# A conformer/S5/MoE decoder trunk on one core: VectorE instead of TensorE forms four modulation tiles during the feed-forward stage

## The reference, cut to what matters

```python
D_MODEL, SEQ, DEPTH = 1024, 256, 2          # BATCH 1, D_FF_DENSE 2816
cond = jax.nn.silu(c.astype(F32))           # c: (1, 1024)
h = x                                       # (1, 256, 1024)
for i in range(DEPTH):
    mod = cond @ mod_w[i].astype(F32) + mod_b[i].astype(F32)        # (1, 6 * 1024)
    sh1, sc1, g1, sh2, sc2, g2 = jnp.split(mod[:, None, :], 6, axis=-1)
    y = rms_norm(h, norm1_g[i]) * (1.0 + sc1) + sh1
    y = conformer_conv(y, ...) if i == 0 else s5_layer(y, ...)
    h = h + g1 * y
    y = rms_norm(h, norm2_g[i]) * (1.0 + sc2) + sh2
    y = (silu(y @ w_gate) * (y @ w_up)) @ w_down if i == 0 else moe_swiglu(y, ...)   # top 2 of 8 experts
    h = h + g2 * y
return rms_norm(h, final_norm_g)
```

## Time and profile before

| | |
|---|---|
| median of 3 runs | 1613.69 us (1611.99 to 1618.89) |
| the profiled execution's own time | 1611.64 us |
| its span | 1608.9 us |
| mean granted clock of TensorE | 0.975 |
| TensorE busy (PE) | 1514.5 us, 94% |
| VectorE busy (DVE) | 1286.9 us, 80% |
| ScalarE busy (ACT) | 1023.9 us, 64% |
| GpSimd busy (POOL) | 217.3 us, 14% |
| instructions | 23502 |

### The profile page before, as it was taken

How to read it: one execution, slowest core, us unless ns; L and a number is a source line. 1 busy time by engine, 2 the same in 40 slices (tenths; PEclk the granted TensorE clock), 3 DMA queues, 4 the chain that set the end, 5 groups by cost and what they waited for, 6 DMA issues and landing times.

```text
span 1608.9 us, 23502 instructions
## 1 busy us (share of the span) xinstructions
PE 1514.5 (94%) x8591; PEld 1260.1 (78%) x8591; DVE 1286.9 (80%) x1426; ACT 1023.9 (64%) x1045; POOL 217.3 (14%) x251
## 2 busy tenths in 40 slices
PE   6997999998889699999999999999989999999996
PEld 4776899998659678888888888888877777777774
DVE  4796566556875598898899889889868988899886
ACT  4556555455123487687777687777748777778773
POOL 0771146521770000000000000000000000000000
PEclk9998999999789899999999999999999999999998
DMA  9954386656484689999999999999818999999991
GB/s 307 331 195 168 106 284 231 236 193 236 158 262 148 220 315 367 361 340 370 363 341 357 374 350 355 365 351 354 306 53 314 340 338 344 340 313 338 376 379 40
DMA packets 231208, 463.30 MB, mean 288 GB/s; under 512 B 18255, under 2 KB 57687, under 8 KB 231127
## 3 DMA queue, kind: packets, MB, share of 16 engines
q1 hardware_dynamic: 229591, 461.55, 80.6%
q10 hardware_dynamic: 1536, 0.68, 0.2%
HBM read 461.15 MB, written 1.05 MB: 287 GB/s over the span
## 4 chain that ended last, share of the span: by engine, by line
PE 75%; DVE 11%; ACT 4%; POOL 4%; issue 3%; DMA 1%; SPq 1%; DVEq 0%; ACTq 0%; POOLq 0%
PE bank L2163 12%; PE bank L2166 12%; PE bank L2169 12%; PE bank L1823 12%; DVE wlo L1744 4%; PE bank L1978 3%; PE bank L2305 3%; PE bank L2302 3%; PE bank L2257 2%; PE bank L2258 2%; PE bank L2265 2%; PE bank L2270 2%; PE bank L2269 2%; DVE bank L1315 2%; PE bank L1907 2%
## 5 line engine op out<-in xcount | busy, mean ns | idle before, releaser
L1597 DVE TENSOR_TENSOR wlo<-ring,whi 128x2048 fp32r<-128x2048 f32 x210 | 477.0, 2289 | 68.5 <-PE bank L2169 55.6
L1020 ACT ACTIVATE whi<-ring 128x2048 fp32r<-128x2048 f32 x210 | 400.9, 1918 | 117.7 <-PE bank L2166 117.7
L1744 DVE TENSOR_TENSOR wlo<-ring,whi 128x2048 fp32r<-128x2048 f32 x126 | 283.1, 2281 | 26.2 <-PE bank L2270 25.0
L1117 ACT ACTIVATE whi<-ring 128x2048 fp32r<-128x2048 f32 x126 | 238.4, 1912 | 37.7 <-PE bank L2265 22.9
L2163 PE MATMUL bank<-whi,xe_hi 128*128 128x512 f32 x560 | 219.7, 392 | 7.2 <-ACT whi L1020 7.2
L2166 PE MATMUL bank<-whi,xe_lo 128*128 128x512 f32 x560 | 218.9, 391 | 0.0
L1233 DVE TENSOR_TENSOR ring_lo<-ring,ehi 128x2048 fp32r<-128x2048 f32 x45 | 106.3, 2362 | 58.3 <-ACT ehi L786 58.2
L2169 PE MATMUL bank<-wlo,xe_hi 128*128 128x512 f32 x560 | 150.5, 391 | 0.0
L2163 PEld LDWEIGHTS bank<-whi,xe_hi 128*128 128x128 f32 x560 | 105.8, 189 | 29.4 <-issue 7.3
L2169 PEld LDWEIGHTS bank<-wlo,xe_hi 128*128 128x128 f32 x560 | 105.7, 189 | 22.1
L2166 PEld LDWEIGHTS bank<-whi,xe_lo 128*128 128x128 f32 x560 | 105.8, 189 | 21.9
(11 more groups left out here) (450 smaller groups left out, 2829.4 us busy)
## 6 DMA issues: line engine op xcount, KB each, us to landing
ring<-in_moe_w_gate_dram SPq DMA_DIRECT2D x112, 1024.0 KB, 7.1
ring<-in_moe_w_up_dram SPq DMA_DIRECT2D x112, 1024.0 KB, 6.8
ring<-in_moe_w_down_dram SPq DMA_DIRECT2D x112, 1024.0 KB, 6.7
ring<-in_mod_w_dram SPq DMA_DIRECT2D x24, 2048.0 KB, 9.8
ring<-in_ffn_w_gate_dram SPq DMA_DIRECT2D x11, 1024.0 KB, 6.1
ring<-in_ffn_w_up_dram SPq DMA_DIRECT2D x11, 1024.0 KB, 8.7
ring<-in_ffn_w_down_dram SPq DMA_DIRECT2D x11, 1024.0 KB, 5.2
ring<-in_conv_w_pw_dram SPq DMA_DIRECT2D x8, 1024.0 KB, 12.3
```

Source lines behind the costliest of these rows:

```text
L1020: act.activation(whi[:, n % HI_SLOTS, :], ring[:, s * HW:(s + 1) * HW], ACT.Copy).then_inc(hi_ready, 1)
L1117: act.activation(whi[:, q % HI_SLOTS, :], ring[:, s * HW:(s + 1) * HW], ACT.Copy).then_inc(hi_ready, 1)
L1597: v.tensor_tensor(wlo[:, n % LO_SLOTS, :], ring[:, s * HW:(s + 1) * HW], whi[:, n % HI_SLOTS, :].bitcast(F32), ALU.subtract).then_inc(lo_r ...
L1744: v.tensor_tensor(wlo[:, q % LO_SLOTS, :], ring[:, s * HW:(s + 1) * HW], whi[:, q % HI_SLOTS, :].bitcast(F32), ALU.subtract).then_inc(lo_r ...
```

## The change

VectorE computes tiles 12 to 15. It multiplies the 512 columns of each of the 8 row tiles by that row tile's values of `cond_late`, one per partition, and adds them up in PSUM bank 6, in 8 steps (`mod_products`); the last step writes to SBUF, where `mod_copy` used to write. The first four steps stand behind `hid_lo` of half 2b, the last four behind `hid_lo` of half 2b+1, ahead of the tables. TensorE's `mod_partial` and ScalarE's `mod_copy` of these tiles are gone. `mod_sums` stays on TensorE, now against a column of ones, and moves from the end of block b to the end of block b+1; `mod_vector` moves likewise. `mod_part`, on which SP waits for the tile's slot, is now counted up by VectorE's last step. The counts of `mod_acc` behind these tiles are four lower (`copies_after`).

```diff
@@ -468,6 +468,13 @@
         S5_TABLE_ORDER = [(2 * m + k) * 4 + q for m in range(4) for q in range(4) for k in range(2)]
         TABLES_AT = [0, 4, 4] + [3] * 8
 
+        def by_vector(m):
+            return 2 * FFN_MODS <= m < 2 * S5_MODS
+
+        def copies_after(m):
+
+            return m - sum(by_vector(k) for k in range(m))
+
         def mod_place(m):
 
             if m < 2 * FFN_MODS:
@@ -933,16 +940,13 @@
                     if f >= 4:
                         act.wait_ge(down_used, f - 3)
                     act.activation(hid_hi[:, f % 4, :], hid[:, f % 4, :], ACT.Copy).then_inc(hidhi_ready, 1)
-                if b in FFN_MOD_BLOCKS:
-                    m = 2 * FFN_MODS + FFN_MOD_BLOCKS.index(b)
-                    mod_copy(m)
                 for n in range(TABLES_AT[b]):
                     if 0 < b < FBLOCKS - 1 and n == TABLES_AT[b] - 1:
                         split_hi(UNIT[("down", b - 1, 0)] + 2)
                     sin_tables(made)
                     made += 1
-                if b in FFN_MOD_BLOCKS and m % 2:
-                    mod_vector(m // 2)
+                if b - 1 in FFN_MOD_BLOCKS[1::2]:
+                    mod_vector(FFN_MODS + FFN_MOD_BLOCKS.index(b - 1) // 2)
 
             squares(hT, sq, h3_ready, lambda kc: kc + 1)
             root(3)
@@ -1356,6 +1360,24 @@
             mod_bias(NORM_MODS + 1)
 
 
+            def mod_products(m, kcs):
+
+                n = WHERE[("mod", m)]
+                w, acc_, dst = early(n, KC), psum[6][:, :], mod_place(m)[2]
+                for kc in kcs:
+                    cc = cond_late[:, kc, 0:1]
+                    if kc == 0:
+                        v.wait_ge(cond_ready, 2)
+                        v.wait_ge(mod_acc, 2 * FFN_MODS)
+                        v.wait_ge(arr[slot_of(n)], arrived_count(n))
+                        link(v.tensor_scalar(acc_, w[:, kc, :], cc, None, ALU.mult))
+                    elif kc < KC - 1:
+                        link(v.scalar_tensor_tensor(acc_, w[:, kc, :], cc, acc_, ALU.mult, ALU.add))
+                    else:
+                        v.wait_ge(mod_sum, m)
+                        v.scalar_tensor_tensor(dst, w[:, kc, :].rearrange("p (a n) -> p a n", a=2), cc,
+                                               acc_.rearrange("p (a n) -> p a n", a=2), ALU.mult, ALU.add).then_inc(mod_part, 1)
+
             made = 0
             for b in range(FBLOCKS):
                 for f in (2 * b, 2 * b + 1):
@@ -1368,6 +1390,8 @@
                     v.wait_ge(hidhi_ready, f + 1)
                     v.tensor_tensor(hid_lo[:, f % 4, :], hid[:, f % 4, :], hid_hi[:, f % 4, :].bitcast(F32),
                                     ALU.subtract).then_inc(hidlo_ready, 1)
+                    if b in FFN_MOD_BLOCKS:
+                        mod_products(2 * FFN_MODS + FFN_MOD_BLOCKS.index(b), range(4 * (f % 2), 4 * (f % 2) + 4))
                 for _ in range(TABLES_AT[b]):
 
                     i = S5_TABLE_ORDER[made]
@@ -1899,7 +1923,7 @@
                 bank = mod_place(m)[0]
                 pe.wait_ge(arr[slot_of(n)], arrived_count(n))
                 if m >= 2:
-                    pe.wait_ge(mod_acc, m - 1 if 2 <= m < 2 * FFN_MODS else m)
+                    pe.wait_ge(mod_acc, m - 1 if 2 <= m < 2 * FFN_MODS else copies_after(m))
                 w, cc = early(n, KC), cond if m < 2 * FFN_MODS else cond_late
                 for first in (True, False):
                     for j in range(4):
@@ -1914,10 +1938,13 @@
                 k, h = m // 2, m % 2
                 if k and h == 0:
                     pe.wait_ge(mod_raw, k)
-                pe.wait_ge(mod_acc, m + 1)
+                if by_vector(m):
+                    pe.wait_ge(mod_part, m + 1)
+                else:
+                    pe.wait_ge(mod_acc, copies_after(m + 1))
                 for o in range(4):
                     ins = mm(bank[:, 4 * h + o:4 * h + o + 1], part[:, o // 2, (o % 2) * P:(o % 2) * P + P],
-                             sum_col[:, :], start=True, stop=True)
+                             ones[:, 0:1] if by_vector(m) else sum_col[:, :], start=True, stop=True)
                 ins.then_inc(mod_sum, 1)
 
             def mod_tiles(first, last):
@@ -1992,15 +2019,11 @@
                         ins = split_product(psum[4 + f % 2][:, g * T:(g + 1) * T], u, y_hi, g,
                                             2 if f == 0 and g == 0 else None)
                     ins.then_inc(gu_done, 1)
-                if b in FFN_MOD_BLOCKS:
-                    m = 2 * FFN_MODS + FFN_MOD_BLOCKS.index(b)
-                    pe.wait_ge(cond_ready, 2)
-                    pe.wait_ge(var_ready, 3)
-                    mod_partial(m)
                 if b:
                     down(b - 1)
-                if b in FFN_MOD_BLOCKS:
-                    mod_sums(m)
+                if b - 1 in FFN_MOD_BLOCKS:
+                    pe.wait_ge(var_ready, 3)
+                    mod_sums(2 * FFN_MODS + FFN_MOD_BLOCKS.index(b - 1))
             down(FBLOCKS - 1)
             pe.wait_ge(mod_raw, S5_MODS)
             sums(3 * KC, sq_ready, sq, sum_ready)
```

## The result

| | before | after |
|---|---|---|
| median | 1613.17 us (5 runs, 1611.93 to 1618.89) | 1629.39 us (5 runs, 1626.77 to 1630.66) |
| ratio | | 1.0094, 95% interval 1.0078 to 1.0109: 15 us slower |
| span of the profiled execution | 1608.9 us | 1628.6 us |
| mean granted clock | 0.975 | 0.963 |

One of the eight executions of the kernel with four steps in half 2 (under Experiments) took 2517.89 us at a mean granted clock of 0.555, and its figures leave that one out.

A forecast was written before the change was run, and what follows sets the result against it. The prediction took the feed-forward stage as TensorE-bound and serial. Its terms, 0 + 3.0 + 1.7 + 2.9 = +7.6 us, plus 3.4 for the clock, gave +11.0 on 1611.64: 1623 us, range 1615 to 1631.

The forecast's parts named there:

- Points 1 to 3: Feed-forward stage: TensorE loses 7.40 us, VectorE gains steps of 0.78 us, its chain comes 3.3 us late against 0.7 slack.
- point 2: Steps added to VectorE: 0.78 us each, 3.1 us for four, from a 746 ns row rather than a 698 ns estimate.
- Point 4: Blocks 6 and 8: stretch 20.1 us against 20.2, change 0, as the removed 1.85 us comes back as a wait.
- Point 5: Block 2: chain held by GpSimd, end of unit 2 at 254.8 instead of 251.8, change +3.0 us.
- Point 6: Block 4: chain held by GpSimd at hid_lo of half 1, stretch 21.9 us against 20.2, change +1.7 us.
- Point 7: Four sums of 0.79 us move into blocks 3, 5, 7 and 9, where TensorE is the bound: +2.9 us.
- Point 8: TensorE's clock: one half-rate spell each in blocks 2 and 4, none in 6 and 8, +3.4 us, bounds 0 and 6.8.
- Point 9: DMA: tile slots freed later, nothing counted, at worst 1 us in each of the four blocks.
- only shifted: All stages behind the feed-forward stage would start later but otherwise stay unchanged.
- Rival A: Waits come but no clock spells, or steps take 0.70 us: +5 to +8, 1616.5 to 1619.5 us; chance 0.24.
- rival C: Faster: the last four steps hide, leaving only the 7.40 us removed from TensorE, 1604 us; chance 0.07.
- B's late transfers: Rival with everything late, 1630 us: transfers late by 1 us per block (4 more), spells in all four blocks; chance 0.11.

The follow-up runs named there:

- the kernel with four steps in half 2: Changed kernel without row tiles 3 to 6 of the four modulation tiles, its four steps per tile all in half 2; 1620.78 us, ratio 1.0041.
- The run with the clock kept up: Changed kernel plus idle TensorE passes at the old place, three portions in block 2, two in 4, one in 6 and 8; 1622.09 us, ratio 1.0051.
- the run with the tables first: Changed kernel with the last four steps behind the tables, ahead of the block's last ring_lo, nothing left out; 1619.38 us, ratio 1.0031.

## Why the prediction was right, and where a size was off

The direction, the place and the mechanism were right, and the time lay in the range; against the 11.0 us forecast, the measured difference was 15.

- Points 1 to 3. TensorE's 7.4 us vanish in waits of its own: shown by putting them back, which costs nothing in blocks 6 and 8 and nothing on balance in the stage. Steps 743 to 755 ns (0.75 taken). The estimate of 698 ns that point 2 works out from the Trainium skill (page "VectorE: DVE Perf Modes", section "Side-by-side: where the cycles go for N=2048 bf16") was 0.05 us too low; the trace's row of 746 was right.
- Point 4, blocks 6 and 8: 20.1 forecast, 20.34 and 20.14 measured.
- Point 5, block 2: 23.2 us (+3.0) without the clock. The run with the clock kept up has 23.12 (+2.9).
- Point 6, block 4: 21.9 forecast, 22.10 with the clock up. One cause there I did not foresee: GpSimd's products now met ring_lo of half 1 rather than hid_lo (4.26 us instead of 2.65), and down waited 0.8 us for it, the last row of the waits after. That the end came out nearly the same is luck.
- Point 7, the moved sums: +2.9 forecast; 0.5 + 3 x 0.9 = 3.1 measured.
- Point 8, the clock: 3.4 forecast, 1.1 + 2.5 = 3.6 measured, but the parts were wrong. Each spell was longer than those of the earlier trace rows, 6.8 us (0.66 over ten us from 290 to 300 is that), and in block 2 part of it fell into the wait, where it is free. The two errors nearly cancel, so the close sum is luck. Nor does the length of a single wait decide, as point 8 took it: in the kernel before, TensorE also waited 2.17 us before 1185.50, and the granted clock from 1185 to 1190 stayed at 1.00. Blocks 6 and 8 kept the clock with all 8 steps, and lost it once with four in half 2: the 350 to 395 row.
- Point 9, DMA: nothing counted, nothing seen, and room even for 3 us more, as the run with the tables first shows.
- Sum of points 1 to 9: 11.0 forecast for the stage, 11.7 measured.
- **The step that failed** is the sentence that the stages behind would be "only shifted". The rest after S5 was; S5 itself was 2.0 to 4.5 us longer in the changed kernel's two profiles, at a lower granted clock, and that term was missing from the sum. It can make up most of what lies between the 11.0 forecast and the 15 measured; why the clock was lower is open.
- Rival A put at 0.24 and rival C at 0.07 fell: the spells came, and the steps did not hide. B's late transfers did not come.

## What to carry to other kernels

An engine that is idle for a third of a stage can still be without free time at the place where the new work stands, if it is a link of a chain that feeds the bound engine there: read the chain into the bound engine, take its slack (0.7 us here), and lay the new work into the gaps where the helper engine waits itself. The same 32 instructions made this kernel 0.9% slower in two blocks of four and 0.3% faster in pairs. Work taken off the bound engine was worth nothing where something else was late, which can be tested by putting idle work of the same length back.

## What the runs showed of the hardware that I had not expected

- Idle TensorE work can pay: 13 us of it made the changed kernel's feed-forward part 3.6 us shorter, because the granted clock stayed at 2.4 GHz in blocks 2 and 4, where with waits of 3.8 us, and of 2.1 and 1.1 us, it fell to 1.2 for 6.8 us each. One portion of 1.85 us in block 2 was too little: the clock fell all the same, and the block was 1.5 us longer.
- The S5 stage, with the same instructions, took 94.8 to 99.3 us over the profiles here, at a mean granted clock of 0.86 to 0.81, and 96.8 and 99.3 in two profiles of one kernel. A difference of some microseconds between single executions can so come from a stage that the change does not touch.
- Vector steps that read an SBUF tensor and a PSUM bank were not slowed beside a GpSimd product: three of them from 236.60 us took 2.34 us with one running from 235.69 for 2.48 us, and 2.33 to 2.34 elsewhere. ring_lo, with two SBUF operands, took 4.26 us instead of 2.29 at 273.66 us, beside a product from 273.36 for 2.41 us.
